# LayerNorm squares of a hybrid Hyena/MLA block: seven adds on GpSimd ahead of one ones matmul, in place of eight accumulating matmuls

## The chip, the core and the metric

The kernel is one program on one core of one Trainium2 chip. The metric is the device time of one launch in microseconds (us), shown as the median of several runs. The engines are named as the profile names them: PE is TensorE's matmul and PEld its weight load, DVE is VectorE, ACT is ScalarE, POOL is GpSimd, SP is SyncE.

## The reference

Two layers work on 1024 latent tokens and 256 context tokens with 1024 channels. Layer 0 mixes with a gated long convolution, layer 1 with multi-head latent attention; each has a SwiGLU feed-forward part. Each of these four sub-layers ends in a LayerNorm over the channels, and this is what the change touches:

```python
def layer_norm(x, g, b):
    xf = x.astype(jnp.float32)
    mu = xf.mean(-1, keepdims=True)
    var = jnp.square(xf - mu).mean(-1, keepdims=True)
    return ((xf - mu) * lax.rsqrt(var + LN_EPS) * g + b).astype(x.dtype)

for i in range(2):                       # cs, the context, goes the same way in layer 0
    yx = hyena_mixer(hx, ...) if i == 0 else attend_blocks(...) @ mla_wo
    xs = layer_norm(ALPHA * xs + g1 * yx, ln_g[i, 0], ln_b[i, 0])
    xs = layer_norm(ALPHA * xs + g2 * swiglu(xs * (1.0 + sc2) + sh2, wg, wu, wd), ln_g[i, 1], ln_b[i, 1])
```

## The kernel before

All activations lie with channels on the 128 partitions, in eight channel tiles (KD = 8), and tokens along the free dimension. The residual is `Ra` or `Rb`, 128 x 8 x tokens. Tokens are worked on in chunks: 512, 512 and 256 in layer 0 (C = 3), 512 and 512 in layer 1 (C = 2). Nearly all matmuls are done in a split form, `mm3` (lines 546 to 548): high part times high part, high times low, low times high.

A sum over channels is a sum over partitions and over the eight tiles. `ones` is a 128x128 constant (one over the channel count), and a matmul with it sums the partitions and hands the sum to all of them. While a sub-layer's last matmuls run, VectorE already adds the eight tiles of the residual into one (`sum_a` to `sum_d`, `add_sum`, line 586), so that the mean costs one ones matmul for each chunk (line 612). The variance does not do this: its squares are summed by eight ones matmuls that accumulate in one PSUM bank.

The four norms are `norms[0]` to `norms[3]`, called norm 0 to norm 3 below. Each engine has its own program, in a fixed order, and semaphores join them:

- VectorE (`norm_dve`) centres a chunk in four operations of two channel tiles each (line 638, residual minus the mean in PSUM), all chunks first. Then, for each chunk, it takes the reciprocal of the standard deviation (line 645) and multiplies in four operations (line 650).
- ScalarE (`norm_act`) squares each centred pair of tiles into one of four buffers `sq[h]`, each 128 x 2 x 512 (line 669). The four buffers are shared by all chunks: the squares of chunk c wait on `norm_var_full` until TensorE has read buffer h of chunk c - 1. Its order with two chunks is squares of 0, squares of 1, root of 0, root of 1 (line 677), then `high(0)`, `high(1)`. With three chunks it is squares of 0 and 1, root of 0, squares of 2, root of 1, `high(0)`, root of 2, `high(1)`, `high(2)`. `high` makes the input of the next sub-layer `ht` (line 695) and its high part (line 700); in norm 3 it makes the output tile (line 686), eight operations a chunk, and SP stores it.
- TensorE (`norm_pe`) does the means and then the variances (line 619).
- GpSimd (`norm_pool`) subtracts the high part from `ht` to get the low part, eight operations a chunk (line 720), and then rewrites the residual (line 725). The next sub-layer's matmuls wait for line 720, chunk by chunk. In norm 1, ScalarE also waits for the end of line 725. In norm 3 GpSimd has nothing to do.

The work of the four norms is not overlapped with the sub-layers around it: the norm needs the last output tile, and the next sub-layer needs the norm.

Of the kernel before, what the change touches and what calls it, by code (L numbers as in the profile page):

```python
# [24 lines left out]
ALU = mybir.AluOpType  # L25
# [5 lines left out]
L_X = 1024  # L31
L_C = 256
T_ALL = L_X + L_C
CHUNKS = {T_ALL: [(0, 512, 0), (512, 512, 0), (1024, 256, 1)], L_X: [(0, 512, 0), (512, 512, 0)]}
# [134 lines left out]
def build(nc, a, out):  # L169
# [21 lines left out]
    with ctx:  # L191
        def sem(name):
            return ctx.enter_context(nc.semaphore(name))

        def sb(stack, name, shape, dt=F32):
            return stack.enter_context(nc.sbuf_tensor(name, shape, dt))
# [10 lines left out]
        ones = sb(ctx, "ones", [P, P])  # L207
# [51 lines left out]
        with ExitStack() as s:  # L259
            Rb = sb(s, "Rb", [P, KD, T_ALL])  # L260
# [58 lines left out]
        scr_a, scr_b, scr_c = (sq_a, st_a, ht_a), (sq_b, st_b, ht_b), (sq_c, st_c, ht_c)  # L319
# [32 lines left out]
        class Stream:  # L352
# [6 lines left out]
            def __init__(self, name, t0):  # L359
                self.t0 = t0  # L360
                self.full = sem(f"{name}_chunk_done")
                self.free = [sem(f"{name}_set{i}_emptied") for i in range(2)]

        class Norm:

            mu, d, sq = sem("norm_mean_full"), sem("norm_centred"), sem("norm_squared")
            var, std, rs = sem("norm_var_full"), sem("norm_std"), sem("norm_rstd")
            n, ht, hi, h = sem("norm_normed"), sem("norm_h_made"), sem("norm_h_high"), sem("norm_h_split")
            r = sem("norm_residual_ready")

            def __init__(self, c0, residuals):
                self.c0, self.residuals = c0, residuals

            def summed(self, m, c, C):

                return m * C + (KD * self.c0 + self.residuals // KD + c + 1)

# [17 lines left out]
        norms = [Norm(c0, KD * (i + 1)) for i, c0 in enumerate((0, 3, 6, 8))]  # L395
# [72 lines left out]
        def bank(i, n=512):  # L468
            return ps[:, i, 0:n]
# [17 lines left out]

        def split_hi(act, sm, t, h, C, first):

            act.wait_ge(sm.raw[h], (t + (sm.t0 + 1)) * 16)  # L490
            if not first:
                act.wait_ge(sm.full, (t * 2 + (h - 1)) * C)
            act.activation(whi[h][:], wraw[h][:], ACT.Copy).then_inc(sm.hi, 1)  # L493
# [15 lines left out]
        def stream_act(act, sm, tiles, T, evac, unroll=False):  # L509

            C = len(CHUNKS[T])

            def body(i, first, last):
                for j in range(2):
                    if not (last and j == 1):
                        split_hi(act, sm, i * 2 + (j + 1), 0, C, False)
                        split_hi(act, sm, i * 2 + (j + 1), 1, C, False)
# [86 lines left out]
        def norm_pe(pe, nm, S, scr, T):  # L604
            C = len(CHUNKS[T])
            ch = CHUNKS[T]
            sq = scr[0]

            def mean(c):
                t0, n, _ = ch[c]  # L610
                pe.wait_ge(s_sum, nm.summed(KD - 1, c, C))
                pe.matmul(bank(c, n), ones[:], S[:, t0:t0 + n], start=True, stop=True).then_inc(nm.mu, 1)

            def var(c):
                t0, n, _ = ch[c]
                for h in range(4):
                    pe.wait_ge(nm.sq, 4 * (nm.c0 + c) + h + 1)
                    for k in range(2):
                        mm = pe.matmul(bank(3 + c, n), ones[:], sq[h][:, k, 0:n],  # L619
                                       start=(h == 0 and k == 0), stop=(h == 3 and k == 1))  # L620
                    mm.then_inc(nm.var, 1)
            for c in range(C):
                mean(c)
            for c in range(C):
                var(c)
# [88 lines left out]
        def norm_pool(pool, nm, idx, R, Hs, scr, T, then=None):  # L714

            C = len(CHUNKS[T])
            for c, (t0, n, _) in enumerate(CHUNKS[T]):
                for k in range(KD):
                    pool.wait_ge(nm.hi, KD * (nm.c0 + c) + k + 1)
                    pool.tensor_tensor(Hs[:, k, 1, t0:t0 + n], scr[2][k % 4][:, 0:n],  # L720
                                       Hs[:, k, 0, t0:t0 + n].bitcast(F32), ALU.subtract).then_inc(nm.h, 1)
            for k in range(KD):
                pool.wait_ge(nm.ht, KD * (nm.c0 + C - 1) + k + 1)
                r = R[:, k, 0:T]
                pool.tensor_scalar(r, r, der[:, idx, 4, k:k + 1], der[:, idx, 5, k:k + 1], ALU.mult, ALU.add
                                   ).then_inc(nm.r, 1)
                if then:
                    then(k)
# [174 lines left out]
        n = dict(A=0, B=0, w1=0, g=0, zn=0)  # L903
# [216 lines left out]
        @block.gpsimd  # L1120
        def _(pool):
            def mod_load(i):

                for t in range(6):
                    pool.wait_ge(s_mu, (i * 6 + (t - 5)) * 2)
                    pool.dma_start(mring[t][:], a["mod_w"][bass.ds(i * 6 + t, 1)].rearrange("o p d -> p (o d)")
                                   ).then_inc(s_mr[t], 16)


            steps = 0  # L1130
            for layer, rows in enumerate((64, P)):
                pool.wait_ge(s_fa, NFC * (layer + 1))
                x, u = fa[0:rows, :], fu[0:rows, :]
                for op in (lambda: pool.tensor_scalar(u, x, MAGIC, None, ALU.add),
                           lambda: pool.tensor_scalar(u, u, -MAGIC, None, ALU.add),
                           lambda: pool.tensor_tensor(x, x, u, ALU.subtract)):
                    op().then_inc(s_fc, 1)
                    steps += 1
                    pool.wait_ge(s_fc, steps)
                pool.tensor_scalar(x, x, TURN_MAX, -TURN_MAX, ALU.min, ALU.max).then_inc(s_fr, 1)  # L1140
                if layer == 0:
                    mod_load(3)
            with pool.Fori(4, 16) as i:
                mod_load(i)

            def spill(k):
                if k >= 1:
                    pool.wait_ge(norms[0].r, k)
                    pool.dma_start(r_dram[:, k - 1, :], Ra[:, k - 1, :]).then_inc(s_rsp, 16)
            norm_pool(pool, norms[0], 0, Ra, Hs0, scr_a, T_ALL, spill)  # L1150
            pool.wait_ge(norms[0].r, KD)
            pool.dma_start(r_dram[:, KD - 1, :], Ra[:, KD - 1, :]).then_inc(s_rsp, 16)
            pool.wait_ge(p_gu[0].full, 4 * NF * 3)
            pool.wait_ge(s_rsp, 16 * KD)
            pool.dma_start(Rb[:], r_dram).then_inc(s_rld, 16)

            norm_pool(pool, norms[1], 1, Rb, HsM, scr_b, T_ALL)
            pool.wait_ge(norms[1].r, norms[1].residuals)
            pool.dma_start(r_dram[:, :, 0:L_X], Rb[:, :, 0:L_X]).then_inc(s_rsp, 16)
            pool.wait_ge(s_rsp, 16 * (KD + 1))  # L1160
            pool.wait_ge(s_sf, HEADS * 8)
            pool.dma_start(Rb[:, :, 0:L_X], r_dram[:, :, 0:L_X]).then_inc(s_rld, 16)
            norm_pool(pool, norms[2], 2, Rb, Hs1, scr_c, L_X)


        @block.scalar
# [839 lines left out]
```

## Time and profile before

| what | value |
|---|---|
| median of 3 runs | 4180.45 us (4176.59 to 4181.89) |
| span of the profiled execution, first to last instruction | 4175.4 us |
| median less that span | 5.0 us |
| PE busy | 3742.1 us, 90% |
| DVE, ACT, POOL busy | 1936.2, 1195.8, 213.4 us |
| mean granted TensorE clock | 0.954 of full speed |

The span is that of one execution. Nothing more exact than the median of other runs is at hand for the time outside the span, so a change of the span is read as a change of the time. The busy shares say which engine works most over the whole program; which engine sets the pace inside a norm has to be read from the order of time in that stretch.

### The profile page before, as it was taken

Reading aid. Unit: us, or ns where it says so; the run is one execution under the profiler, and the core shown is the slowest. Engines: PE = TensorE matmul, PEld = TensorE weight load, DVE = VectorE, ACT = ScalarE, POOL = GpSimd, SP = SyncE. Lnnn points to the kernel's source line nnn. Section 1 sums busy time; section 2 is a strip of 40 time slices with the busy share of each in tenths; the row PEclk is TensorE's granted clock in tenths of the full one; section 3 lists DMA queues with packets and bytes.
Section 4 is the critical chain, followed back from the end, with each engine's and each line's share of the span. In section 5 each row is a group of like instructions: output and inputs, shape, how many; then the busy total and the mean of one; then the engine's idle time right before and its main releaser. Section 6 shows DMA issues by size and latency. Waiting matters only on the chain.

```text
span 4175.4 us, 48044 instructions
## 1 busy us (share of the span) xinstructions
PE 3742.1 (90%) x17670; PEld 2999.3 (72%) x17670; DVE 1936.2 (46%) x2738; ACT 1195.8 (29%) x1904; POOL 213.4 (5%) x189
## 2 busy tenths in 40 slices
PE   2999589888887979999999978899999879999997
PEld 0888376566665858888878857677677758888775
DVE  8899544434445441111135561555555441111556
ACT  2221223322323041111134452333333241111444
POOL 4111000000000040000000021000000030000000
PEclk9999789988998989999999989999999989999999
DMA  5565633444333121111121102000000201111111
GB/s 193 180 200 199 189 81 86 103 101 89 81 99 123 46 73 38 38 38 38 39 82 36 38 20 74 7 13 6 6 18 0 76 28 48 49 49 48 43 46 63
DMA packets 161726, 290.61 MB, mean 70 GB/s; under 512 B 15095, under 2 KB 87607, under 8 KB 161079
## 3 DMA queue, kind: packets, MB, share of 16 engines
q1 hardware_dynamic: 147016, 229.50, 19.2%
q0 software_dynamic: 14608, 59.77, 4.1%
q8 instruction: 60, 0.98, 0.1%
q14 instruction: 42, 0.34, 0.0%
HBM read 196.94 MB, written 29.36 MB: 54 GB/s over the span
## 4 chain that ended last, share of the span: by engine, by line
PE 79%; DMA 7%; DVE 7%; POOL 2%; ACT 2%; issue 1%; SPq 1%; DVEq 0%; ACTq 0%; POOLq 0%
PE ps L546 20%; PE ps L547 20%; PE ps L548 20%; PE ps L1451 7%; DMA t2k<-s 3%; DMA t2z<-s 3%; PE ps L1511 2%; PE ps L1460 2%; PE ps L1471 2%; POOL Hs L720 1%; DVE mx L1895 1%; PE ps L619 1%; PE ps L1402 1%; PE ps L1546 1%; PE ps L1410 1%
## 5 line engine op out<-in xcount | busy, mean ns | idle before, releaser
L546 PE MATMUL ps<-Hs,whi 128*128 128x512 f32 (+1 forms) x2528 | 927.8, 367 | 100.0 <-DVE Hs L1665 47.2
L547 PE MATMUL ps<-Hs,whi 128*128 128x512 f32 (+1 forms) x2528 | 926.0, 366 | 0.0
L548 PE MATMUL ps<-Hs,wlo 128*128 128x512 f32 (+1 forms) x2528 | 924.0, 366 | 0.0
L498 DVE TENSOR_TENSOR wlo<-wraw,whi 128x512 fp32r<-128x512 f32 x268 | 191.5, 716 | 924.3 <-ACT whi L493 919.3
L546 PEld LDWEIGHTS ps<-Hs,whi 128*128 128x128 f32 x2528 | 480.5, 190 | 184.5 <-issue 87.8
L547 PEld LDWEIGHTS ps<-Hs,whi 128*128 128x128 f32 x2528 | 480.9, 190 | 75.9
L548 PEld LDWEIGHTS ps<-Hs,wlo 128*128 128x128 f32 x2528 | 479.8, 190 | 77.3
L493 ACT ACTIVATE whi<-wraw 128x512 fp32r<-128x512 f32 x268 | 168.7, 632 | 1271.1 <-PE ps L548 1218.3
L546 PE MATMUL ps<-ghi,whi 128*128 128x512 f32 (+1 forms) x880 | 330.8, 376 | 26.5 <-DVE Rb L821 12.8
L836 DVE TENSOR_TENSOR glo<-G,ghi 128x1280 fp32r<-128x1280 f32 (+1 forms) x176 | 237.6, 1357 | 221.6 <-ACT ghi L782 221.3
L547 PE MATMUL ps<-glo,whi 128*128 128x512 f32 (+1 forms) x880 | 330.0, 375 | 0.0
L548 PE MATMUL ps<-ghi,wlo 128*128 128x512 f32 (+1 forms) x880 | 328.0, 373 | 0.0
L782 ACT ACTIVATE ghi<-G 128x1280 fp32r<-128x1280 f32 (+1 forms) x176 | 203.9, 1166 | 291.3 <-PE ps L548 291.3
L546 PEld LDWEIGHTS ps<-ghi,whi 128*128 128x128 f32 x880 | 168.8, 192 | 61.6 <-DVE Rb L821 14.7
L1451 PE MATMUL ps<-t2k,st 128*128 128x256 f32 x640 | 180.0, 407 | 33.0 <-DMA t2z<-s 19.9
L1240 ACT ACTIVATE pq<-ps 128x512 f32<-128x512 f32 x160 | 95.5, 597 | 357.9 <-PE ps L1451 357.9
L548 PEld LDWEIGHTS ps<-ghi,wlo 128*128 128x128 f32 x880 | 168.0, 191 | 29.9
L547 PEld LDWEIGHTS ps<-glo,whi 128*128 128x128 f32 x880 | 168.8, 192 | 27.9
L1765 DVE TENSOR_TENSOR prod<-ps,pq 128x512 f32<-128x512 f32 x160 | 110.7, 692 | 154.6 <-PE ps L1451 154.6
L1451 PE MATMUL ps<-t2z,st 128*128 128x256 f32 x640 | 174.2, 397 | 0.0
L1451 PEld LDWEIGHTS ps<-t2k,st 128*128 128x128 f32 x640 | 129.5, 205 | 54.8 <-issue 24.6
L1232 ACT ACTIVATE s<-ps 128x512 f32<-128x512 f32 x160 | 95.5, 597 | 250.0 <-DMA t2k<-s 109.2
(216 smaller groups left out, 5446.9 us busy)
## 6 DMA issues: line engine op xcount, KB each, us to landing
wraw<-in_w_gu SPq DMA_DIRECT2D x176, 256.0 KB, 2.6
mring<-in_mod_w POOLq DMA_DIRECT2D x78, 512.0 KB, 4.5
wraw<-in_w_d SPq DMA_DIRECT2D x88, 256.0 KB, 2.6
t2k<-s SPq DMA_DIRECT2D x160, 128.0 KB
t2z<-s SPq DMA_DIRECT2D x160, 128.0 KB
t2w<-w SPq DMA_DIRECT2D x160, 128.0 KB
wraw<-in_w_in SPq DMA_DIRECT2D x48, 256.0 KB, 4.4
u_scratch<-uo SPq DMA_DIRECT2D x24, 512.0 KB, 2.6
```

The costliest lines, as they stand in the source:

```text
L493: act.activation(whi[h][:], wraw[h][:], ACT.Copy).then_inc(sm.hi, 1)
L498: dve.tensor_tensor(wlo[h][:], wraw[h][:], whi[h][:].bitcast(F32), ALU.subtract).then_inc(sm.lo, 1)
L546: pe.matmul(o, wh, xh, start=start, stop=False)
L547: pe.matmul(o, wh, xl, start=False, stop=False)
L548: return pe.matmul(o, wl, xh, start=False, stop=stop)
L782: act.activation(ghi[G_SLOT[f]][:, 0:T], G[:, f, 0:T], ACT.Copy).then_inc(dn.ghi, 1)
L836: dve.tensor_tensor(glo[G_SLOT[f]][:, 0:T], G[:, f, 0:T], ghi[G_SLOT[f]][:, 0:T].bitcast(F32), ALU.subtract).then_inc(dn.glo, 1)
L1232: act.activation(s1[slot % 3][:].rearrange("p a b -> p (a b)"), bank(BANK_B[slot % 2]), ACT.Copy).then_inc(s_be, 1)
L1240: act.activation(pq[q % 2][:].rearrange("p a b -> p (a b)"), bank(BANK_C[q % 2]), ACT.Copy).then_inc(s_pq, 1)
L1451: mm = pe.matmul(ps[:, bk, CW * (b % 2):CW * (b % 2) + CW], blk, src[:, g, :], start=True, stop=True)
L1460: mm = pe.matmul(ps[:, BANK_A[au % 2], CW * ((g - 1) % 2):CW * ((g - 1) % 2) + CW], mi[:, g0 + g - 1, :], ysb[(q - 1) % 2][:], start=True, ...
L1765: dve.tensor_tensor(prod[:].rearrange("p a b -> p (a b)"), bank(BANK_D[q % 2]), pq[q % 2][:].rearrange("p a b -> p (a b)"), ALU.mult).then ...
```

## The change

In every norm the squares of a chunk are no longer summed over the channel tiles by accumulating matmuls. GpSimd does it in place in the square buffers: four adds of the two tiles inside a buffer (waiting for one ScalarE square each), two adds across buffers, and a last one. One ones matmul then sums `sq[0][:, 0]`. The semaphore on which ScalarE waits before it writes the buffers again is raised by four at once, behind that one matmul. GpSimd adds all chunks of a norm before it begins its old work in that norm, and gets a part in norm 3.

```diff
@@ norm_pe @@
             def var(c):
                 t0, n, _ = ch[c]
-                for h in range(4):
-                    pe.wait_ge(nm.sq, 4 * (nm.c0 + c) + h + 1)
-                    for k in range(2):
-                        mm = pe.matmul(bank(3 + c, n), ones[:], sq[h][:, k, 0:n],
-                                       start=(h == 0 and k == 0), stop=(h == 3 and k == 1))
-                    mm.then_inc(nm.var, 1)
+                pe.wait_ge(nm.part, 7 * (nm.c0 + c) + 7)
+                pe.matmul(bank(3 + c, n), ones[:], sq[0][:, 0, 0:n], start=True, stop=True).then_inc(nm.var, 4)
@@ norm_pool @@
+            def add_squares(c):
+
+                n = CHUNKS[T][c][1]
+                at = 7 * (nm.c0 + c)
+                for h in range(4):
+                    pool.wait_ge(nm.sq, 4 * (nm.c0 + c) + h + 1)
+                    pool.tensor_tensor(sq[h][:, 0, 0:n], sq[h][:, 0, 0:n], sq[h][:, 1, 0:n], ALU.add
+                                       ).then_inc(nm.part, 1)
+                for h in (0, 2):
+                    pool.wait_ge(nm.part, at + h + 2)
+                    if h == 2:
+                        pool.wait_ge(nm.part, at + 5)
+                    pool.tensor_tensor(sq[h][:, 0, 0:n], sq[h][:, 0, 0:n], sq[h + 1][:, 0, 0:n], ALU.add
+                                       ).then_inc(nm.part, 1)
+                pool.wait_ge(nm.part, at + 6)
+                pool.tensor_tensor(sq[0][:, 0, 0:n], sq[0][:, 0, 0:n], sq[2][:, 0, 0:n], ALU.add).then_inc(nm.part, 1)
+            for c in range(C):
+                add_squares(c)
+            if Hs is None:
+                return
@@ the GpSimd program @@
             norm_pool(pool, norms[2], 2, Rb, Hs1, scr_c, L_X)
+            norm_pool(pool, norms[3], 3, Rb, None, scr_c, L_X)
```

How the rows stand on the engines. First TensorE in norm 3, at the end of the program; `sum_d` is the sum of the residual's tiles, `sqc` are the square buffers. Before:

```order
L612 MATMUL ps<-sum_d,ones 128x512 [waits channel_sum_added] x2
L619 MATMUL ps<-sqc,ones 128x512 [waits norm_squared]
L619 MATMUL ps<-sqc,ones 128x512
L619 MATMUL ps<-sqc,ones 128x512 [waits norm_squared]
L619 MATMUL ps<-sqc,ones 128x512
L619 MATMUL ps<-sqc,ones 128x512 [waits norm_squared]
L619 MATMUL ps<-sqc,ones 128x512
L619 MATMUL ps<-sqc,ones 128x512 [waits norm_squared]
L619 MATMUL ps<-sqc,ones 128x512
```

and eight rows more of the same kind for the second chunk. After:

```order
L613 MATMUL ps<-sum_d,ones 128x512 [waits channel_sum_added] x2
L618 MATMUL ps<-sqc,ones 128x512 [waits norm_squares_added] x2
```

Sixteen matmuls, every second one behind a square, have become two, each behind the last of seven adds.

GpSimd in norms 2 and 3; line 720 (739 after) makes the low parts, line 725 (744 after) rewrites the residual. Before:

```order
L1162 DMA Rb<-residual_scratch 128x8x1024 [waits scores_full,residual_spilled]
L720 TENSOR_TENSOR Hs<-htc,Hs 128x512 [waits norm_h_high] x16
L725 TENSOR_SCALAR Rb<-Rb,der 128x1024 [waits norm_h_made] x8
L191 UNCONDITIONAL_BRANCH
```

After (the six rows of adds of norm 3, between line 744 and the last row, repeat the six of norm 2):

```order
L1181 DMA Rb<-residual_scratch 128x8x1024 [waits scores_full,residual_spilled]
L722 TENSOR_TENSOR sqc<-sqc 128x512 [waits norm_squared] x4
L728 TENSOR_TENSOR sqc<-sqc 128x512 [waits norm_squares_added] x2
L731 TENSOR_TENSOR sqc<-sqc 128x512 [waits norm_squares_added]
L722 TENSOR_TENSOR sqc<-sqc 128x512 [waits norm_squared] x4
L728 TENSOR_TENSOR sqc<-sqc 128x512 [waits norm_squares_added] x2
L731 TENSOR_TENSOR sqc<-sqc 128x512 [waits norm_squares_added]
L739 TENSOR_TENSOR Hs<-htc,Hs 128x512 [waits norm_h_high] x16
L744 TENSOR_SCALAR Rb<-Rb,der 128x1024 [waits norm_h_made] x8
```

Fourteen adds stand ahead of line 720's work in norm 2 and fourteen in norm 3; norms 0 and 1 have 21 each, seven of them 256 wide.

ScalarE's order is the same in both kernels. Its end in norm 3, before:

```order
L669 ACTIVATE sqc<-Rb 128x1024 [waits norm_centred] x4
L669 ACTIVATE sqc<-Rb 128x1024 [waits norm_var_full,norm_centred] x4
L677 ACT_TABLE_LOAD
L677 ACTIVATE stdc<-ps,eps_t 128x512 [waits norm_var_full] x2
L686 ACTIVATE Rb<-Rb,vecs 128x512 [waits norm_normed] x16
```

After, the same rows stand there under other line numbers. What `norm_var_full` stands for has moved: it is raised by four behind a chunk's only matmul, where it was raised by one behind each pair.

## Rows read from the trace of the kernel before

**Rows 1.** The page: busy time, share and instructions by engine; then the ending chain.
```profile
PE 3742.1 (90%) x17670; PEld 2999.3 (72%) x17670; DVE 1936.2 (46%) x2738; ACT 1195.8 (29%) x1904; POOL 213.4 (5%) x189
...
PE 79%; DMA 7%; DVE 7%; POOL 2%; ACT 2%; issue 1%; SPq 1%; DVEq 0%; ACTq 0%; POOLq 0%
```

**Rows 2.** Chain that ended last, norm 3: start us, us, engine, tile, line.
```profile
4139.06 2.09 PE ps L612 x2
4141.17 1.23 DVE Rb L638
4142.43 1.06 ACT sqc L669
4143.53 7.15 PE ps L619 x16
4150.76 1.06 ACT sqc L669
4151.84 1.28 ACT L677
4153.13 0.70 ACT stdc L677
4153.85 3.37 DVE stdc L645
4157.24 1.09 DVE Rb L650
```

**Rows 3.** ScalarE in order of time, norm 2: start, us, engine, line, what, count, idle before.
```profile
3357.58 7.84 ACT L669 ACTIVATE sqc<-Rb 128x1024 f32<-128x1024 f32 x7 [2.70 <-DVE Rb L638]
...
3373.66 1.52 ACT L695 ACTIVATE htc<-Rb,der 128x512 f32<-128x512 f32 x2 [0.24 <-DVE Rb L650]
```

**Rows 4.** VectorE and GpSimd in order of time, norm 2.
```profile
3372.40 4.63 DVE L650 TENSOR_TENSOR Rb<-Rb,stdc 128x1024 f32<-128x1024 f32 x4
3376.95 3.35 DVE L645 RECIPROCAL stdc<-stdc 128x512 f32<-128x512 f32 x1
3380.33 7.98 DVE L650 TENSOR_TENSOR Rb<-Rb,stdc 128x1024 f32<-128x1024 f32 x4
...
3375.78 24.72 POOL L720 TENSOR_TENSOR Hs<-htc,Hs 128x512 fp32r<-128x512 f32 x16 [132.83 <-ACT Hs L700]
```

**Rows 5.** Line 720: operations with ns min/median/max, all of norm 0, then 1488.2 to 1496.1.
```profile
L720 POOL TENSOR_TENSOR Hs<-hta,Hs x24: 716/1258/2252, 1484.9 to 1516.2; 128x512 fp32r<-128x512 f32 x16, 128x256 fp32r<-128x256 f32 x8
...
L720 POOL TENSOR_TENSOR Hs<-hta,Hs x5: 1260/2243/2252, 1488.2 to 1496.1; 128x512 fp32r<-128x512 f32 x5
```

**Rows 6.** GpSimd in order of time, the filter arguments at the program's start.
```profile
25.99 6.66 POOL L1135 TENSOR_SCALAR fu<-fu 64x2560 f32<-64x2560 f32 x1
32.73 5.56 POOL L1136 TENSOR_TENSOR fa<-fa,fu 64x2560 f32<-64x2560 f32 x1
38.38 3.17 POOL L1140 TENSOR_SCALAR fa<-fa 64x2560 f32<-64x2560 f32 x1
```

**Rows 7.** Ones matmuls: norm 3's mean (ns min/median/max; in time), then variances.
```profile
L612 PE MATMUL ps<-sum_d,ones x4: 937/1057/1219, 4139.1 to 4141.8; 128*128 128x512 f32 x4
...
4139.06 3.66 PE L612 MATMUL ps<-sum_d,ones 128*128 128x512 f32 x4 [4.34 <-DVE sum_d L586]
...
L619 PE MATMUL ps<-sqc,ones x64: 592/592/697, 3358.7 to 4156.9; 128*128 128x512 f32 x64
```

**Rows 8.** Stretches: us; busy PE, PEld, DVE, ACT, POOL; granted clock, DMA share, GB/s.
```profile
2460.00:2478.00 18.00, 17.45 (x48) 9.04 (x48) 16.81 (x16) 14.88 (x19) 0.41 (x1) 1.00 0.01 6
3400.00:3405.00 5.00, 4.45 (x11) 3.52 (x12) 0.00 (x0) 0.00 (x0) 5.00 (x5) 0.50 0.00 0
4139.00:4143.00 4.00, 3.66 (x4) 1.12 (x4) 3.19 (x5) 0.57 (x1) 0.00 (x0) 0.57 0.01 2
4143.00:4158.00 15.00, 14.00 (x32) 6.00 (x32) 11.42 (x9) 10.27 (x11) 0.00 (x0) 1.00 0.00 0
```

**Rows 9.** In order of time, norms 0 and 1: first squares, half-wide squares, line 720.
```profile
1464.78 5.58 ACT L669 ACTIVATE sqa<-Ra 128x1024 f32<-128x1024 f32 x5 [2.17 <-DVE Ra L638]
...
1484.90 31.99 POOL L720 TENSOR_TENSOR Hs<-hta,Hs 128x512 fp32r<-128x512 f32 x24 [1041.84 <-ACT Hs L700]
...
2459.16 7.84 ACT L669 ACTIVATE sqb<-Rb 128x1024 f32<-128x1024 f32 x7 [8.57 <-DVE Rb L638]
...
2470.46 1.14 ACT L669 ACTIVATE sqb<-Rb 128x512 f32<-128x512 f32 x2
...
2474.91 0.67 ACT L677 ACTIVATE stdb<-ps,eps_t 128x512 f32<-128x512 f32 x1
...
2477.59 31.99 POOL L720 TENSOR_TENSOR HsM<-htb,HsM 128x512 fp32r<-128x512 f32 x24 [357.81 <-ACT HsM L700]
```

More of the change, by code:

```diff
@@ L369, in build @@
             r = sem("norm_residual_ready")
+            part = sem("norm_squares_added")
             def __init__(self, c0, residuals):
@@ L716, in norm_pool @@
             C = len(CHUNKS[T])
+            sq = scr[0]
+            def add_squares(c):
[17 more added lines that the diff above has]
+                return
             for c, (t0, n, _) in enumerate(CHUNKS[T]):
```

## The prediction

> **What bounds the kernel now.** I read the page first. TensorE is busy 90% of the span and holds 79% of the chain that ended last [rows 1], so work taken from TensorE would gain if it lay in a stretch that TensorE bounds. The ones matmuls of the variance are such work only by name: they lie inside the norms, where the sub-layers' matmuls stand still and a chain through several engines sets the pace. So the second view is the chain in norm 3, in order of time [rows 2]: mean, centring, one square, then 7.15 us of ones matmuls, another square, the load of the root's table, the root, the reciprocal. The reader is to see that the ones matmuls are a link there, but one that runs beside the squares. The four squares of chunk 0 start 7.84/7 = 1.12 us apart [rows 3], and the matmuls follow one square behind. They also hand the buffers back one by one, so that the last square of chunk 1 ends 9.4 us after the first square of chunk 0 began (4151.8 less 4142.4) and the first root ends at 11.4 [rows 2]. What the change must beat is these 9.4 and 11.4 us.
>
> In norms 0 to 2 the end is set by GpSimd's line 720: it begins when the first high part is ready and then runs without a pause [rows 4, 9], and the next sub-layer waits for its last chunk. What counts there is by how much line 720 starts later. Counted from the first square it starts at 20.1 us in norm 0, 18.4 in norm 1 [rows 9] and 18.2 in norm 2 [rows 3, 4].
>
> **The change part by part.** Removed: the eight ones matmuls of a chunk, 16 records of 7.15 us in all [rows 2]. The cover is already there, so what goes from the path is only what stuck out behind the squares.
>
> Added: seven adds a chunk on GpSimd. The trace has no such add. The nearest row is line 720, two inputs in SBUF, 512 wide: 1.26 us when alone, about 2.24 when VectorE's line 650 runs beside it [rows 5]. The other near row is the filter's subtraction of 2560 elements in 5.56 us, which is 1.11 us for 512 [rows 6]. I take 1.26 (same width, same engine, same count of inputs), with 1.11 and 2.24 as ends. A GpSimd operation that waits for the one before it starts 0.08 us behind its end [rows 6]; the second and third add across buffers do that. Half-wide adds: 0.73, as the shortest of line 720 is 0.716 [rows 5].
>
> Which of the ends holds beside VectorE's centring (line 638)? What the rows show is that line 650 suffers and makes suffer: four of them take 7.98 us beside line 720 and 4.63 alone, while the reciprocal takes its 3.35 us in the middle of line 720 [rows 4]. Line 650 has both inputs in SBUF, line 638 has one of them in PSUM, the reciprocal has one input. I take line 638 to be like the reciprocal. The Trainium skill, SBUF — State Buffer, "Who interferes with whom", says the same: a VectorE instruction with two SBUF inputs contends with GpSimd's reads, one with at most one outside the 2-port modes does not. By that rule the trace's 7.98 against 4.63 is explained and the centring stays clear; no row of this kernel shows line 638 beside GpSimd.
>
> Added too: one ones matmul, two records. TensorE idles some 9 us before it. After 4.3 us without work [rows 7] the mean of norm 3 ran at a granted clock of 0.57 (the 1.2 GHz level most of the time), and its two records took 2.09 us [rows 2, 8]; in the long row of variance matmuls the clock was 1.00 (2.4 GHz) [rows 8] and a record 0.59 us, about 1.0 for two [rows 7]. I take 2.1, with 1.0 as the other end.
>
> Norm 3, from the first square (time 0). Squares end at 1.06, 2.2, 3.3, 4.4. GpSimd is slower than the squares: in-buffer adds end at 2.4, 3.7, 4.9, 6.2, those across at 7.4, 8.8, 10.1. The matmul ends at 12.3. Only now may ScalarE overwrite the buffers: squares of chunk 1 from 12.35 to 16.8 where they ended at 9.4. Table load and root (1.28 and 0.69) follow, and the first root ends at 18.8 where it ended at 11.4: **+7.4**. The reciprocals and scalings behind it are a chain of their own (reciprocal, four scalings, reciprocal, first scaling), and the second root, at 25.4, is there before its reciprocal would start at 26.8. So the output moves by +7.4.
>
> Norm 2. Behind the same start, GpSimd adds chunk 1 from 13.5 to 22.5 (squares 1.12 apart, adds 1.26), the matmul ends at 24.7 and the second root at 25.4. In ScalarE's order the second root stands ahead of `high(0)`; this is what is queued behind the new wait. `high(0)` began at 16.1 [rows 3] and now begins at 25.4: **+9.3**, and line 720 with it. GpSimd has finished its adds by then.
>
> Norms 0 and 1. Squares of chunk 2 wait for the matmul of chunk 1: 24.75 to 27.05 (half wide, 1.14 for two [rows 9]). Root of chunk 1 ends at 27.7, and the first high part is ready at about 29.7, since line 720 started 2.7 us after that root began [rows 9]. But GpSimd must first add chunk 2: from 25.45, 7 x 0.73 + 0.2 = 5.3, and some 0.5 for the overlap with line 650, so until 31.3. Line 720 starts there: 31.3 - 20.1 = **+11.2** in norm 0 and 31.3 - 18.4 = **+12.9** in norm 1. In norm 1 ScalarE also waits for line 725 behind it, which moves by the same.
>
> Line 720's own length I leave as it is: VectorE's scalings move with it and overlap it as before. Nothing hides these shifts, since the sub-layers' matmuls have nothing else to do. Sum: 7.4 + 9.3 + 11.2 + 12.9 = 40.8 us on a span of 4175.4, or **4221.3** on the median of 4180.45.
>
> The low end of this case takes 1.11 an add and 1.0 for the matmul: first root at +5.3, `high(0)` of norm 2 at 21.3 (+5.2), line 720 in norms 0 and 1 at 25.9 (+5.8, +7.5), together 23.8, so 4204. The high end takes the half-wide adds of chunk 2 beside line 650 at one microsecond more for four of them (+3.5 in each of two norms) and one more low-clock start of the sub-layer behind norm 0, where 5 us at 0.50 [rows 8] cost 2.5: 50, so 4231.
>
> A rule against the change: GPSIMD Engine Reference of the Trainium skill, "3.1 Elementwise", gives about 2.6 cycles an element at 1.2 GHz for a two-input operation, from which I estimate 1.11 us for 512. The row of line 720 at 1.26 is a little above it. By the page the sum would be some 7 us less (0.15 us on seven adds, for one full chunk in norm 3 and two in the others), and still slower.
>
> **The rivals.**
> First, *contention with the centring*. If line 638 is like line 650 after all, the adds of chunk 0 cost 2.24 each while VectorE centres. For it: the adds of chunk 0 lie fully beside the centring, and 2.24 is a measured pair. Against it: the PSUM operand. Price: four adds +3.9 us, all seven +6.9, in each of four norms, +16 to +27 over the forecast: 4237 to 4249.
>
> Second, *relief for line 720*. If it starts so late that part of line 650 is over, it loses up to the 1 us on each of the four overlapped operations, in norms 0 to 2: 12 us at most, 4209 to 4221. Against it: the second scaling starts at 30 in my norm 2, with line 720 at 27.5.
>
> Third, the other side, *not slower: adds that cost nearly nothing*, as if the filter's width were all that one pays for. With adds of zero length chunk 0's variance is ready at 5.5, squares of 1 end at 10.0 against 9.4, the root is 0.6 late, and line 720 begins within 0.4 us of where it did in norms 1 and 2 and 1.5 earlier in norm 0, whose ones matmuls began at the low clock. The four nearly cancel: 4180. It decides only below some 0.2 us an add; the lowest row shows 1.11. A gain of over 8 us has no mechanism that I can find: even free adds leave the squares of chunk 1 behind those of chunk 0.
>
> **How the numbers follow.** Forecast 0.79, contention 0.12, relief 0.05, not slower 0.04. The range runs from the forecast case's low end, 4204, over its high end to the lower edge of the contention case, 4237; it leaves out most of that case and the last, under 2 in 10. Within 0.2%, about what a measurement of this kernel can tell from no change, is 4172 to 4189: 0.03 of the last rival's 0.04 lie there and 0.01 below it; the other cases, 0.96 together, are all slower.
>
> **What would show it.** In the profile after: line 731's adds about 10 us after the first square; squares of chunk 1 waiting some 8 us on TensorE's line 618; adds of 1.26 us and centring unchanged at 1.23 [rows 2] (2.2 on both means the first rival); line 739 first at 27.5 us in norm 2 and 31 in norms 0 and 1, and about 24.7 and 32 us long. TensorE's busy time falls, though the span grows. Wrong would be an add far from 1.26, or a square of chunk 1 that begins before chunk 0's matmul has ended.

## The result and the profile after

The changed kernel takes 4220.2 us (median of 4 runs, 4213.35 to 4230.15), the one before 4178.64 us on the same chip (4 runs, 4176.59 to 4181.89). The ratio is 1.010, with a 95% interval of 1.0084 to 1.0116: 42 us or 1% slower. The prediction was 4221.3.

The page of the kernel after: busy time, share and instructions by engine, then the chain that ended last [rows 1 of before].

```profile
span 4211.7 us, 47854 instructions
PE 3690.1 (88%) x17530; PEld 2970.3 (71%) x17530; DVE 1937.2 (46%) x2738; ACT 1194.1 (28%) x1904; POOL 292.5 (7%) x259
...
PE 78%; DMA 7%; DVE 6%; POOL 4%; ACT 2%; issue 2%; SPq 1%; DVEq 0%; ACTq 0%; POOLq 0%
```

TensorE lost 52 us of busy time and 140 records, GpSimd won 79 us and 70 instructions, and the span grew by 36.3 us (4211.7 less 4175.4; the spans are of one execution each, the 42 us of the medians). In the ending chain GpSimd's share went from 2% to 4%. Where the time went shows in norm 3, in the chain that ended last, in order of time (start, us, engine, tile, line), against [rows 2]:

```profile
4167.93 2.09 PE ps L613 x2
4170.04 1.23 DVE Rb L635
4171.30 1.07 ACT sqc L666
...
4172.43 4.97 POOL sqc L722 x4
4177.40 1.24 POOL sqc L728
...
4178.78 1.27 POOL sqc L728
...
4180.12 1.27 POOL sqc L731
...
4181.52 2.06 PE ps L618 x2
...
4184.63 2.93 ACT sqc L666 x3
4187.58 1.28 ACT L674
4188.87 0.70 ACT stdc L674
4189.59 3.36 DVE stdc L642
```

The reader is to see the squares of chunk 1 behind the matmul of chunk 0. From the first square (4171.30) it is 12.3 us until they begin and 18.3 until the first root has ended, where it was 11.4. ScalarE's own order of time in norm 2 shows the two waits, against [rows 3]:

```profile
3378.82 4.45 ACT L666 ACTIVATE sqc<-Rb 128x1024 f32<-128x1024 f32 x4 [2.70 <-DVE Rb L635]
3391.17 3.90 ACT L666 ACTIVATE sqc<-Rb 128x1024 f32<-128x1024 f32 x4 [7.91 <-PE ps L618]
3395.09 1.28 ACT L674 ACT_TABLE_LOAD   x1
3396.38 0.69 ACT L674 ACTIVATE stdc<-ps,eps_t 128x512 f32<-128x512 f32 x1
3403.44 0.69 ACT L674 ACTIVATE stdc<-ps,eps_t 128x512 f32<-128x512 f32 x1 [6.37 <-PE ps L618]
3404.03 1.51 ACT L692 ACTIVATE htc<-Rb,der 128x512 f32<-128x512 f32 x2
```

Eight squares that ran in one piece of seven and one are now two pieces of four with 7.9 us between them, and `high(0)` (line 692) stands behind a second root that comes 6.4 us late.

To read each norm by itself, whatever the stages between do in one execution, I take the time from the norm's first square to the end of GpSimd's low parts (norms 0 to 2) or to the end of the span (norm 3). All are differences of two times in one trace. In the kernel before they are 52.1, 50.4, 42.9 and 33.0 us; the table gives what each kernel adds. "Ratio" is the timed ratio to before on the same chip with its 95% interval. e4, e6 and e7 have none: they ran once, in 4189.96, 4169.6 and 4228.27 us, where before had medians of 4181.13, 4178.48 and 4178.48.

| kernel | norm 0 | norm 1 | norm 2 | norm 3 | sum, us | ratio |
|---|---|---|---|---|---|---|
| after | +10.7 | +12.3 | +8.0 | +7.4 | +38.4 | 1.010 (1.0084 to 1.0116) |
| e1, adds in norm 3 only | 0.0 | 0.0 | +2.8 | +7.4 | +10.2 | 1.003 (1.0012 to 1.0048) |
| e2, buffers handed back at the end | +2.8 | +4.5 | +2.8 | +4.8 | +14.9 | 1.0033 (1.0011 to 1.0055) |
| e8, adds left out | -0.6 | +1.1 | +1.3 | +1.2 | +3.0 | 0.9999 (0.9977 to 1.0022) |
| e3, two sets of buffers | +6.8 | +8.5 | +5.4 | +4.2 | +24.9 | 1.0049 (1.0022 to 1.0075) |
| e7, first root first | +13.8 | +15.5 | +12.3 | +11.1 | +52.7 | |
| e4, pairs only | -0.9 | -0.1 | 0.0 | +0.3 | -0.8 | |
| e6, early table only | -0.9 | +0.9 | +1.3 | +1.0 | +2.3 | |
| e5, pairs and early table | -2.4 | -1.3 | -1.2 | -1.2 | -6.1 | 0.9979 (0.9964 to 0.9994) |
| e9, before with the root early | -2.8 | -1.1 | +0.3 | -1.5 | -5.1 | 0.9972 (0.9959 to 0.9985) |
| e10, e5 and e9 together | +5.8 | +7.2 | -0.7 | +1.3 | +13.7 | 1.0027 (1.0009 to 1.0045) |

The sums lie inside the intervals of the ratios (1% is 41.8 us) for all but e9, whose timed gain is 6 to 17 us. The four norms thus carry the result. In the two traces what lies outside them did not grow: up to the first square of norm 0 it is 1464.8 us before and 1466.0 after, and from the end of one norm's low parts to the next norm's first square 942.3 and 942.4, 848.0 and 845.0, 741.9 and 741.6.

### The profile page after: what moved, and what is told of

Read it like the earlier page. It is cut to its first block, busy times and chain, and to the rows that moved or that the text cites. A ratio compares the mean times of both kernels' runs of the same rounds, so it can differ in the third digit from the quotient of the medians.

```text
span 4211.7 us, 47854 instructions
## 1 busy us (share of the span) xinstructions
PE 3690.1 (88%) x17530; PEld 2970.3 (71%) x17530; DVE 1937.2 (46%) x2738; ACT 1194.1 (28%) x1904; POOL 292.5 (7%) x259
## 4 chain that ended last, share of the span: by engine, by line
PE 78%; DMA 7%; DVE 6%; POOL 4%; ACT 2%; issue 2%; SPq 1%; DVEq 0%; ACTq 0%; POOLq 0%
PE ps L547 20%; PE ps L548 20%; PE ps L549 20%; PE ps L1471 7%; DMA t2k<-s 3%; PE ps L1531 2%; DMA t2z<-s 2%; PE ps L1491 2%; PE ps L1480 2%; POOL Hs L739 1%; DVE mx L1915 1%; PE ps L1422 1%; PE ps L1566 1%; SPq L1082 1%; PE ps L1430 1%
## 5 line engine op out<-in xcount | busy, mean ns | idle before, releaser
L547 PE MATMUL ps<-ghi,whi 128*128 128x512 f32 (+1 forms) x880 | 330.3, 375 | 27.4 <-DVE wlo L859 13.8
```

The lines of the kernel that those rows point to most:

```text
L547: pe.matmul(o, wh, xh, start=start, stop=False)
```

## The experiments

The theory: what costs is a chain. ScalarE's next squares wait for a buffer, the buffer for the one matmul, the matmul for seven adds on GpSimd; and behind ScalarE's late squares stand its roots and `high(0)`. Rival A: TensorE idles more, so its clock is low behind the norms and the sub-layers pay. The stretches just given already speak against it: behind the norms of the changed kernel the sub-layers took no longer than before. Nor did they when counted from their own first matmul to the next norm's first square: 959.5 us before and 959.6 after, 865.2 and 862.2, 751.6 and 751.3. Rival B: the adds are simply long, wherever they stand; handing back the buffers plays no part.

**e1: the adds in norm 3 alone.** The first three norms keep the eight matmuls.

```diff
             def var(c):
                 t0, n, _ = ch[c]
+                if nm.c0 < 8:
+                    ... the eight matmuls of before ...
+                    return
-                pe.wait_ge(nm.part, 7 * (nm.c0 + c) + 7)
+                pe.wait_ge(nm.part, 7 * (nm.c0 - 8 + c) + 7)
...
-            for c in range(C):
+            for c in range(C if Hs is None else 0):
                 add_squares(c)
```

> The adds on GpSimd in norm 3 alone; norms 0 to 2 as before. Theory (a chain of squares, seven adds, a matmul at the low clock, and only then the next squares): norm 3 alone carries 7.4 us, so +7.4 us over before, with the first root ending 18.8 us after the first square. Rival A (an idle TensorE leaves the clock low and the sub-layers behind pay): nothing of norms 0 to 2 is touched, so the same +7 here, but then norms 0 to 2 must carry more than their own shift in the full change. Rival B (GpSimd's adds are simply too long, the hand-back of the buffers plays no part): norm 3 has no other GpSimd work, so the cost is two chunks of what sticks out, 2 us or less.

Norm 3 gave +7.40 us in this trace and +7.43 in that of after; norms 0 and 1 were as before to 0.02 us. So the cost sits where the edit is and does not leak into other norms. The first root ended at 18.3 us, not at 18.8; why the output still moved by 7.4 stands with the account of the prediction. Rival B's 2 us is out. Norm 2, whose code is that of before, took 2.8 us more here; the section on the hardware comes back to that.

**e2: the buffers handed back at the end, without any add.**

```diff
                     for k in range(2):
                         mm = pe.matmul(bank(3 + c, n), ones[:], sq[h][:, k, 0:n],
                                        start=(h == 0 and k == 0), stop=(h == 3 and k == 1))
-                    mm.then_inc(nm.var, 1)
+                mm.then_inc(nm.var, 4)
```

> The kernel before with one edit: the eight matmuls of a chunk raise the semaphore by four behind the last of them and not by one behind each pair. No adds. Theory: the squares of chunk 1 start at 8.3 us and not staggered; the first root ends at 14.7 and not 11.4. +3.3 in norm 3, +3.1 in norm 2, about +3 in norm 1 and +3.4 in norm 0: +13 us. Rival B: TensorE does the same work at the same times, +0 to 2 us.

+14.9 us in the norms. ScalarE in norm 3, in order of time:

```profile
4159.53 4.45 ACT L669 ACTIVATE sqc<-Rb 128x1024 f32<-128x1024 f32 x4 [12.05 <-DVE Rb L638]
4169.80 3.89 ACT L669 ACTIVATE sqc<-Rb 128x1024 f32<-128x1024 f32 x4 [5.81 <-PE ps L619]
```

The same split into two fours with a wait between them, made by one moved semaphore alone, with TensorE's and GpSimd's work untouched. Rival B's "0 to 2" is out again. Norms 1 and 3 were 1.5 us dearer than I expected because the matmuls began at the low clock there: norm 3's 16 records took 9.07 us in the chain, not 7.15 as in [rows 2]. Norms 0 and 2, whose matmuls began as in the kernel before, gave +2.8 each. At that price the four would be +11.4 us, an estimate from these two rows: handing back the buffers in one piece costs by itself some three tenths of what the change costs.

**e8: the adds left out, everything else as in the change.**

```diff
             def var(c):
                 t0, n, _ = ch[c]
-                pe.wait_ge(nm.part, 7 * (nm.c0 + c) + 7)
+                pe.wait_ge(nm.sq, 4 * (nm.c0 + c) + 4)
                 pe.matmul(bank(3 + c, n), ones[:], sq[0][:, 0, 0:n], start=True, stop=True).then_inc(nm.var, 4)
...
-            for c in range(C):
-                add_squares(c)
             if Hs is None:
                 return
```

> The changed kernel with the seven adds of every chunk left out (the variance is that of one channel tile in eight): the one matmul waits for the fourth square. The hand-back of the buffers behind that matmul stays, and TensorE is as idle as with the change. Theory: matmul done at 6.6 us, squares of chunk 1 until 11.0, first root at 13.0 against 11.4: +1.6 in norm 3, +1.4 in norm 2, +1.2 in norm 1, -0.5 in norm 0, in all +4 us over before. So the length of the adds carries nearly all of the cost. Rival A (low clock behind the norms): a good part of the +41 us stays, 15 us or more. The third rival of the prediction had a matmul of 1.0 us here and so +0.

+3.0 us in the norms, and a ratio that can't be told from 1. ScalarE in norm 3:

```profile
4144.42 4.45 ACT L666 ACTIVATE sqc<-Rb 128x1024 f32<-128x1024 f32 x4 [12.08 <-DVE Rb L635]
4151.16 3.89 ACT L666 ACTIVATE sqc<-Rb 128x1024 f32<-128x1024 f32 x4 [2.29 <-PE ps L618]
```

The second four begin 6.7 us after the first square and not 12.3. TensorE has the same work as in the change, but its pause ahead of the first variance matmul is shorter, 4.2 to 5.8 us against 10.1 to 11.5. So it is not quite as idle as the expectation has it, and e8 alone would not settle rival A, which wanted 15 us here; together with the unchanged stretches behind the norms of the change it is out. With e2 this splits the change: the hand-back in one piece costs by what stands in front of it, 2.8 us a norm behind eight matmuls and 1.1 to 1.3 us in norms 1 to 3 behind one. This is also the prediction's third rival in its pure form: adds that take no time leave +3, with a first matmul of about 2.1 us where that rival had 1.0.

**e3: two sets of square buffers.** Set c % 2 for chunk c; the second set of norm 1 lies in `cq` and `ckv`, which are not yet in use.

```diff
+                sq_a += [sb(s2, f"sqa{i}", [P, 2, 512]) for i in range(4, 8)]
...
-                    if c >= 1:
-                        act.wait_ge(nm.var, 4 * (nm.c0 + c - 1) + h + 1)
-                    act.activation(sq[h][:, :, 0:n], R[:, 2 * h:2 * h + 2, t0:t0 + n],
+                    if c >= 2:
+                        act.wait_ge(nm.var, 4 * (nm.c0 + c - 2) + h + 1)
+                    act.activation(sq[4 * (c % 2) + h][:, :, 0:n], R[:, 2 * h:2 * h + 2, t0:t0 + n],
```

> The changed kernel with a second set of four square buffers for odd chunks, so that the squares of chunk 1 wait for nothing and those of chunk 2 for chunk 0. Theory: GpSimd goes from chunk 0's adds to chunk 1's at once (10.2 us) but now beside VectorE's scaling of chunk 0, which has two inputs in SBUF: first root at 13.1, second at about 24. Norm 3 +4.9, norm 2 +8.2, norms 0 and 1 +9.1 and +7.4: about +30 us over before, 10 less than the change. Rival B (the adds alone, wherever they stand): no different from the change, +40.

+24.9 us against +38.4: taking the wait for the buffers away was worth 13.5 us net, the new collisions included, and the rest is the length of the adds and the order behind them. The theory had +30, so the direction is right and the size 5 too large, mostly because norms 2 and 3 came out 2.8 and 0.7 us better. GpSimd and VectorE in norm 3, in order of time, also show a collision:

```profile
4180.57 2.66 POOL L731 TENSOR_TENSOR sqc<-sqc 128x512 f32<-128x512 f32 x2
4183.31 2.12 POOL L734 TENSOR_TENSOR sqc<-sqc 128x512 f32<-128x512 f32 x1
...
4178.68 3.35 DVE L646 RECIPROCAL stdc<-stdc 128x512 f32<-128x512 f32 x1 [5.16 <-ACT stdc L678]
4182.06 6.73 DVE L651 TENSOR_TENSOR Rb<-Rb,stdc 128x1024 f32<-128x1024 f32 x4
```

Beside the reciprocal two adds take 2.66 us, as alone; beside the scaling one takes 2.12 and the four scalings 6.73, not 4.63. I had put three or four adds into that collision; in the trace it is one, since the adds of chunk 1 are nearly over when scaling begins at 16.4 us.

**e7: the root of chunk 0 ahead of the squares of chunk 1.**

```diff
             square(0)
-            square(1)
             for c in range(C - 1):
                 std(c)
+                if c == 0:
+                    square(1)
                 if c + 2 < C:
                     square(c + 2)
```

> The changed kernel with ScalarE's order turned: the root of chunk 0 ahead of the squares of chunk 1. Theory: the first root ends at 13.0 and not 18.3, but the squares of chunk 1 start later, and VectorE's scaling of chunk 0 now falls on GpSimd's adds of chunk 1, both slower; the second root comes at about 28.8 and not 25.3. In norm 3 +2 us over the change, in norm 2 +3 to 4. Rival B: the first root is 5 us earlier and so is what follows, -5 us a norm against the change.

Norm 3 +3.7 and norm 2 +4.3 us against the change, a little more than expected, and +14 in the four norms. ScalarE in norm 3:

```profile
4194.84 0.69 ACT L674 ACTIVATE stdc<-ps,eps_t 128x512 f32<-128x512 f32 x1 [6.56 <-PE ps L618]
4195.42 3.88 ACT L666 ACTIVATE sqc<-Rb 128x1024 f32<-128x1024 f32 x4
4211.46 0.69 ACT L674 ACTIVATE stdc<-ps,eps_t 128x512 f32<-128x512 f32 x1 [12.15 <-PE ps L618]
```

The first root ends at 13.0 us, 5.3 earlier, and the kernel is slower: the second root comes at 29.6 and not 25.3, and `high(0)` waits for it. The collision is there as expected: in norm 3 four of chunk 1's adds took 2.06 to 2.29 us and three of the scalings 2.28. An earlier first root is worth nothing while the second stands ahead of the work that both feed.

**e4, e5 and e6: only the four adds inside the buffers.** GpSimd halves each buffer, four matmuls take the four halves and hand back one buffer each (e4). e5 also has one line ahead of the first square, which loads the root's table while ScalarE waits. e6 is the kernel before with that line alone.

```diff
             def var(c):
                 t0, n, _ = ch[c]
-                pe.wait_ge(nm.part, 7 * (nm.c0 + c) + 7)
-                pe.matmul(bank(3 + c, n), ones[:], sq[0][:, 0, 0:n], start=True, stop=True).then_inc(nm.var, 4)
+                for h in range(4):
+                    pe.wait_ge(nm.part, 4 * (nm.c0 + c) + h + 1)
+                    pe.matmul(bank(3 + c, n), ones[:], sq[h][:, 0, 0:n], start=(h == 0), stop=(h == 3)).then_inc(nm.var, 1)
...
+            act.activation(stds[0][:, 0:1], eps_t[:], ACT.Sqrt)
             square(0)
```

> The pairs on GpSimd with four matmuls, without the early table load. Theory: the first root 1.28 us later than with it, 11.2, line 739 at about 18.3 in norms 1 and 2, as before the change; in sum -1 us against before, where the full seven adds cost +38. Rival B (four of seven adds, so 4/7 of the cost): +22 us.

> The changed kernel with two edits. GpSimd does only the four adds inside the buffers; four ones matmuls sum the four results and hand back one buffer each. And a root of one column is taken ahead of the first square, so that the root's table is loaded while ScalarE waits for the centring. Theory: where a buffer is handed back behind one add and one matmul, the squares of chunk 1 follow almost at once. At the low clock (two records 1.9 us) the first root ends at 11.3, at the high one at 9.6, against 18.3 with the change and 11.4 before. Norms 0 to 2 and 3 each within 2 us of before, in sum between -8 and 0 us. Rival B (GpSimd's adds are too slow for this place at any number): four of seven adds stay, so about 4/7 of the +38, +22 us.

> The kernel before with the root's table loaded early and nothing else, to tell that edit from the pairs. Theory: the first root ends at 10.1 and not 11.4. In norm 3 the output moves by -1.3; in norms 0 to 2 the second root, which waits for TensorE until 15.8, holds high(0), so -0.2 each: -2 us in the four norms.

e4: -0.8 us, against +38.4 with all seven adds. Rival B wanted +22. Four of the seven adds are thus free in this place, where each hands its buffer on at once. What costs in the change is the three adds across buffers together with the single hand-back; how much is due to which, e4 does not say, since it takes both away, and no run has four adds with a single hand-back. It is also one trace, and the kernel was not timed further; e5 bears it out with a timed ratio. e5: -6.1 us and a ratio of 0.9979. ScalarE in its norm 3:

```profile
4146.87 4.45 ACT L667 ACTIVATE sqc<-Rb 128x1024 f32<-128x1024 f32 x4 [10.57 <-DVE Rb L636]
4151.51 1.06 ACT L667 ACTIVATE sqc<-Rb 128x1024 f32<-128x1024 f32 x1 [0.19 <-PE ps L619]
4153.22 2.95 ACT L667 ACTIVATE sqc<-Rb 128x1024 f32<-128x1024 f32 x3 [0.65 <-PE ps L619]
4156.07 0.67 ACT L675 ACTIVATE stdc<-ps,eps_t 128x512 f32<-128x512 f32 x1
```

The squares flow with waits of 0.2 and 0.65 us, and no table load stands between the last square and the root, which ends at 9.9 us. e6 missed: +2.3 and not -2. The table load is gone from the path there too, but the matmuls began at the low clock, and the first root of norm 3 ended at 12.5. The two stretches, its first 4 us of variance matmuls and the rest (us, busy PE, PEld, DVE, ACT, POOL, granted clock, DMA share, GB/s):

```profile
4134.00:4138.00 4.00, 3.31 (x5) 1.45 (x5) 4.00 (x4) 3.78 (x4) 0.00 (x0) 0.50 0.00 0
4138.00:4152.00 14.00, 13.53 (x29) 5.50 (x28) 9.32 (x7) 5.59 (x7) 0.00 (x0) 0.92 0.00 0
```

In the kernel before the same matmuls ran at 1.00 throughout [rows 8]. The clock hid the edit in norms 1 to 3. In norm 0 the first two matmuls took 1.53 us here and 1.59 before, so the clocks were alike: there the first root ended 1.4 us earlier, the low parts began at the same 20.1, nearly as expected, and the norm gave -0.9. e5 against e4 shows the early table better: -5.3 us in the four norms, with the first root 1.4, 1.5, 1.2 and 1.4 earlier. Their first two matmuls took the same time to 0.02 us in norms 0 to 2, and in norm 3 e5's were the slower, 2.08 against 1.13.

**e9: the kernel before, with ScalarE's order turned.** No adds on GpSimd.

```diff
             square(0)
+            std(0)
             square(1)
-            for c in range(C - 1):
-                std(c)
-                if c + 2 < C:
-                    square(c + 2)
-                if c >= 1:
-                    high(c - 1)
-            std(C - 1)
-            high(C - 2)
+            high(0, {5 if idx == 3 else 3: lambda: std(1), **({5: lambda: square(2)} if C == 3 else {})})
+            if C == 3:
+                std(2)
+                high(1)
             high(C - 1)
```

> The kernel before (eight matmuls, no adds) with ScalarE's order turned: root of chunk 0 ahead of the squares of chunk 1, then high(0), with the root of chunk 1 taken behind its third tile (sixth in norm 3) and the squares of chunk 2 behind its fifth. Theory, that ScalarE's order decides what waits: first root at 9.0 and not 11.4, line 720 starts at 15.7 and not 18.2 in norm 2, the output of norm 3 moves by -1.6; GpSimd may run dry once, so -1.5 to -2 in each of norms 0 to 2. In sum -6 us, -0.15%. Rival: GpSimd's low parts set the pace and run dry or collide longer with VectorE, so that the early start is given back, 0 us.

-5.1 us in the norms of its trace, with norm 2 at the low clock (first root at 11.8, in the other three at 9.0), and a ratio of 0.9972 (0.9959 to 0.9985). The interval is a gain of 6 to 17 us, so some of the timed gain has no place in the norms and stays open. Part of norm 0's -2.8 is clock too: its first two matmuls took 1.12 us and not 1.59. The turn that cost 14 us in e7 gains here. The second root now stands inside `high(0)` and not ahead of it, which is my reason for it; but e9 has no adds either, and no run has e7's order with the eight matmuls, so the share of the two is not shown. ScalarE in norm 3:

```profile
4126.80 0.69 ACT L677 ACTIVATE stdc<-ps,eps_t 128x512 f32<-128x512 f32 x1 [2.53 <-PE ps L619]
4127.38 3.88 ACT L669 ACTIVATE sqc<-Rb 128x1024 f32<-128x1024 f32 x4
4132.16 3.63 ACT L688 ACTIVATE Rb<-Rb,vecs 128x512 f32<-128x512 f32 x5 [0.90 <-DVE Rb L650]
4135.70 0.67 ACT L677 ACTIVATE stdc<-ps,eps_t 128x512 f32<-128x512 f32 x1
```

**e10: e5 and e9 together.** The diffs are those two, and one more, which the order of chunks makes necessary: GpSimd adds chunk 2 behind its low parts of chunk 0.

```diff
-            for c in range(C):
+            for c in range(2):
                 add_squares(c)
...
                                        Hs[:, k, 0, t0:t0 + n].bitcast(F32), ALU.subtract).then_inc(nm.h, 1)
+                if c == 0 and C == 3:
+                    add_squares(2)
```

> Pairs on GpSimd with four matmuls, the table loaded early, and ScalarE's order with the root of chunk 0 ahead of the squares of chunk 1; GpSimd adds chunk 2 behind its low parts of chunk 0. Theory: the two gains come from different links of the chain and add up. First root at 8.0, high(0) at 12.6, line 720's work at 14.7 and not 18.2 in norm 2; the output of norm 3 -2.9. About -3 in each norm, -12 us in all, -0.28%. Rival: in norms 0 to 2 GpSimd's low parts set the pace from then on and collide with VectorE for longer, so that only norm 3 gains: -3 us.

A clear miss: +13.7 us. ScalarE and GpSimd in norm 1, in order of time:

```profile
2490.39 1.14 ACT L702 ACTIVATE HsM<-htb 128x512 fp32r<-128x512 f32 x2
2501.16 0.48 ACT L675 ACTIVATE stdb<-ps,eps_t 128x256 f32<-128x256 f32 x1 [9.63 <-PE ps L619]
...
2488.64 7.97 POOL L733 TENSOR_TENSOR HsM<-htb,HsM 128x512 fp32r<-128x512 f32 x4 [0.85 <-ACT HsM L702]
2496.57 2.77 POOL L724 TENSOR_TENSOR sqb<-sqb 128x256 f32<-128x256 f32 x4
2503.64 16.57 POOL L733 TENSOR_TENSOR HsM<-htb,HsM 128x512 fp32r<-128x512 f32 x15 [4.31 <-ACT HsM L702]
```

It is the fault of the change once more, in another place. The root of chunk 2 stands ahead of `high(1)` on ScalarE; it waits for a matmul, that for adds queued behind GpSimd's low parts. ScalarE stands for 9.6 us and then GpSimd for 4.3. Neither the theory nor its rival had named that wait, though it is in the order of instructions. In norm 2, which has no third chunk, the pair gave -0.7 us and not -3. `high(0)` began at 13.4 us there, but GpSimd was still adding chunk 1, two of its adds at 2.25 to 2.29 us beside the scalings, and began the low parts only at 16.7, right behind the last of them. Norm 3 gave +1.3: its first squares' matmuls began late at the low clock, and the first scalings ran beside the adds of chunk 1 (the outputs come in pairs 2.2 us apart).

## Why the prediction was right

**The sum.** 40.8 us forecast, 38.4 found in the four norms, 42 in the timing. That 4220.2 came within 1.1 us of 4221.3 is luck: the four runs lie between 4213 and 4230. What the traces bear out is the chain of waits and its length in each norm. By norm, for the start of line 720's work (739 after), or the output in norm 3:

| | forecast | found | low parts' own length, before and after |
|---|---|---|---|
| norm 0 | +11.2 | +12.5 | 31.99, 30.11 |
| norm 1 | +12.9 | +14.2 | 31.99, 30.08 |
| norm 2 | +9.3 | +9.1 | 24.72, 23.6 |
| norm 3 | +7.4 | +7.4 | |

Norm 3 is exact by two errors that cancel. I had the squares of chunk 1 at 4.45 us, as where they wait for the centring; behind the late hand-back they took 3.90, so the first root ended at 18.3, +6.9 and not +7.4. But the first scaling of chunk 0 then fell beside GpSimd's last add of chunk 1 and took 1.80 us, not 1.23, and the four took 5.21, where they took 4.63 before:

```profile
4192.98 5.21 DVE L647 TENSOR_TENSOR Rb<-Rb,stdc 128x1024 f32<-128x1024 f32 x4
```

**The add.** Taken at 1.26 from line 720: GpSimd in order of time, norms 2 and 0.

```profile
3379.96 4.96 POOL L722 TENSOR_TENSOR sqc<-sqc 128x512 f32<-128x512 f32 x4 [114.67 <-ACT sqc L666]
3384.88 2.66 POOL L728 TENSOR_TENSOR sqc<-sqc 128x512 f32<-128x512 f32 x2
3387.62 1.26 POOL L731 TENSOR_TENSOR sqc<-sqc 128x512 f32<-128x512 f32 x1
...
1491.40 3.97 POOL L722 TENSOR_TENSOR sqa<-sqa 128x256 f32<-128x256 f32 x4 [3.00 <-ACT sqa L666]
1495.33 1.59 POOL L728 TENSOR_TENSOR sqa<-sqa 128x256 f32<-128x256 f32 x2
1497.00 1.68 POOL L731 TENSOR_TENSOR sqa<-sqa 128x256 f32<-128x256 f32 x1
1498.64 30.11 POOL L739 TENSOR_TENSOR Hs<-hta,Hs 128x512 fp32r<-128x512 f32 x24
```

Four in 4.96, three more in 3.9 with the gaps of 0.08: right. Mis-sized was the half-wide group of norms 0 and 1. I put 5.3 + 0.5 = 5.8 us; it took 7.2, since three of its adds fell beside the scalings: two took 1.7 us each and one 0.94, where the other four took 0.72. That is the 1.3 us by which both norms started later than forecast.

**The centring.** The first rival is out. VectorE's line 635 is the centring, now beside the adds of chunk 0 (ns min/median/max):

```profile
L635 DVE TENSOR_TENSOR Rb<-Rb,ps x28: 674/1210/1222, 2469.9 to 4178.0; 128x1024 f32<-128x1024 f32 x24, 128x512 f32<-128x512 f32 x4
L722 POOL TENSOR_TENSOR sqc<-sqc x16: 1257/1269/1280, 3380.0 to 4188.5; 128x512 f32<-128x512 f32 x16
```

Neither side is slower than alone (1.21 and 1.26 us at most 1.22 and 1.28). So a VectorE operation with one input in PSUM did not get in GpSimd's way here, and the rule of the Trainium skill, SBUF — State Buffer, "Who interferes with whom", agrees with this trace on both sides: the scaling with two SBUF inputs collides, as e3 showed again, the centring with one does not.

**The matmul.** Taken at 2.1 us: 2.06 in the chain, at a granted clock of 0.50 (the level of 1.2 GHz; stretch 4181 to 4184, columns as above). The pause ahead of it was 10.1 us, not the 9 that I had put.

```profile
4181.00:4184.00 3.00, 2.05 (x2) 0.50 (x2) 0.00 (x0) 0.34 (x1) 0.38 (x1) 0.50 0.00 0
```

**The relief.** Given 0.05 as a case of its own, it came true as a small term beside the forecast: the low parts were 1.9, 1.9 and 1.1 us shorter. In all three norms they no longer meet the last scaling of chunk 0 (the first of them took 2.38 us in norm 2 before and 1.27 after), and in norms 0 and 1 the first scaling of chunk 1 was over, too, before they began, so that three of them took 2.24 beside full-width scalings of chunk 1 and not four. I had argued that the overlap would be the same. The two errors, +2.6 for the half-wide adds and -4.9 for the relief, partly cancel, which is part of why the sum came out so close.

**The third rival.** Its mechanism was tried in e8 and its premise (adds of no length) is what fails; its time is +3, not 0, by the matmul's clock.

## What to carry to other kernels

Before work is taken from the engine that is busiest over the program, look at what that work waits for and who waits for it where it stands: here 7 us of matmuls ran one step behind the squares and handed the buffers back one by one, and both were lost. A reduction that is moved to another engine should pass its results on as finely as the one it replaces (in e4's one trace four adds and four matmuls cost nothing, seven adds and one matmul cost 38 us), and in an engine's program a wait for the next chunk must not stand ahead of work that the last chunk has already made possible (e7, e10 lost by it, e9 gained).

## What the runs showed of the hardware

The level of TensorE's clock at the start of the variance matmuls is not fixed by the code. Norm 2 has the same instructions before and in e1: its first root ended 11.4 us after the first square in the one and 14.2 in the other. The first 4 us of its squares, before and then e1 (columns as above; 1.00 is the level of 2.4 GHz, 0.50 that of 1.2):

```profile
3358.00:3362.00 4.00, 3.31 (x8) 1.63 (x9) 4.00 (x5) 3.78 (x4) 0.00 (x0) 1.00 0.15 57
3375.00:3379.00 4.00, 3.63 (x5) 1.57 (x6) 4.00 (x5) 3.49 (x4) 0.00 (x0) 0.50 0.09 34
```

In both TensorE had run the matmuls of the mean in the same 1.02 and 1.13 us and had then idled 2.3 us. In norm 3 of e6 the granted clock was 0.50 over the first 4 us, before it was 1.00 [rows 8]; there TensorE had idled 4.35 and 4.34 us, run the means for 3.78 and 3.66, and idled 0.69 and 0.82. That is 1.5 to 3 us a norm, as much as most edits here are worth, so single traces of such a kernel are to be compared norm by norm with the first root's time beside them. What decides the level I have not found out.

The runs of one and the same kernel scatter by more than that: among 17 runs of the kernel before on one chip, the fastest took 4161.89 us at a mean clock of 0.959, the slowest 4196.48 at 0.949. In the traces the norms are not where this comes from. The stretch ahead of norm 0, whose work no edit touches, ended at 1448.5 us in e9 and at 1481.5 in e1, with a granted clock of 0.92 and 0.88 between 400 and 1440 us; the others lie between, at 1464.8 and 0.89 in the kernel before. The three stretches between the norms differ by 1.6, 3.3 and 1.1 us over all twelve traces. So a whole time tells of an edit to the norms only as the median of many runs, and a single trace only norm by norm.
